# The modulation projections of a two-network kernel: all inputs summed in each column quarter, and the block turned on VectorE

## The chip, the cores and the metric

One Trainium2 chip, and one of its NeuronCores. The metric is the device time of one launch in microseconds, of the core that runs it. The kernel before took 2778.16 us (median of 3 runs, 2774.78 to 2778.19).

## The reference

Two small transformer-like networks run one after the other on the same 256 tokens of width 1024, all in fp32. The first has two layers (a gated feed-forward block, a mixer with three branches, a second gated feed-forward block). The second has two layers whose norms are shifted, scaled and gated by vectors made from a condition. The change touches only these vectors:

```python
def adaln(cond, w, b):
    return jnp.split(jax.nn.silu(cond) @ w + b, 6, axis=-1)
...
sh1, sc1, gt1, sh2, sc2, gt2 = [m[:, None, :] for m in adaln(c, w_ada, b_ada)]
csh1, csc1, cgt1, csh2, csc2, cgt2 = adaln(c_ctx, w_ada, b_ada)
```

`c` and `c_ctx` are two vectors of 1024, `w_ada` is 1024 x 6144 for each of two layers. So two rows are multiplied by 12,288 columns; the result is needed with the feature on the partition, since everything else in the kernel is kept that way.

## The kernel before, in words

Each engine has its own instruction list, written out by hand in the order in which it runs; semaphores tie them together. The sections are `load`, `one` (the first network, a loop over 2 layers), `cload`, `ctx`, `kv` and `two`.

The feed-forward blocks of section `one` are done by `multiply(c, which)`, twice per layer (`which` 0 and 1). Each walks through 17 groups of weights (k = 0 to 16; 11 for the way up, 6 for the way down) with a scheme that makes a 2 x 2 block product from 7 products instead of 8. A group's seven products ("quarters", all on L739) are on TensorE in this order: `middle(k)` has three, `raw(k+1)` two, `end(k)` two. Each quarter is 8 matmuls of 128 columns (6 on most of the way down), and each fp32 matmul shows as two passes in the profile, so a row of x16 is a whole quarter. VectorE makes the sums and differences of the weights that the products take (L1771, L1772, L1785, L1791), combines products (L1830 `c11_made`, L1845 `c22_made`, L1852 `c21_made`) and gates or adds the results. ScalarE copies products out of PSUM (L1337 is the line of its helper).

The modulation projections are strewn into these blocks: six in each `multiply`, at k = 1, 4, 7, 10, 13 and 16, so 12 per layer and 24 in all. One of them takes 512 of the 12,288 columns: its weights (2 MB, tile `fox_values_mla_qk_mla_values`, `vqv`) are 8 tiles of 128 inputs x 512 outputs, the condition (`cond_s`) is stationary as 8 tiles of 128 inputs x 32 columns of which two are real. Its steps are:

- TensorE, `ada_sums` (L710), between `middle(k)` and `raw(k+1)`: 8 matmuls of 512 columns. Input tile kt goes to column quarter kt mod 4 of the array, so each quarter of the PSUM partitions holds the sum over 2 of the 8 input tiles, for all 512 outputs.
- ScalarE, `ada_copy`: the 128 x 512 block is copied to SBUF (`ada_s`, in tile `delta_qkv`).
- TensorE, `ada_turn` (L719), after `end(k)`: 4 matmuls with a 128 x 128 piece of the block as the stationary operand and two columns of constants as the moving one; they add up the four quarters and turn the result at once.
- VectorE, `ada_bias` (L1756), last in iteration k: adds the bias into `modulation`.

SyncE's queue holds all the weight loads in one row. The load of a projection (`load_ada`, L565) stands just before the load of the group that shares its k (L595); the first of a layer stands between the loads of groups 0 and 1. It waits for a semaphore `ada_summed` that counts the finished sums; `load_ada` number 6 waits for another signal that the mixer sets. A signal's `at(c, k)` gives the semaphore and the count that k events of this layer stand for, on top of all earlier ones.

Of the kernel before, what the change touches and what calls it, by code (L numbers as in the profile page):

```python
# [21 lines left out]
ALU = mybir.AluOpType  # L22
# [4 lines left out]
P = 128  # L27
# [3 lines left out]
KD = D // P  # L31
# [232 lines left out]
def build(nc, stream, x_in, ctx_in, cond, positions, vec1, vec2, bada, consts, tables, out):  # L264
    with ExitStack() as ctx:
# [116 lines left out]
        ada_loaded = signal("ada_weights_loaded", one=16 * ADA_TURN)  # L382
        ada_summed = signal("ada_summed", 1, one=ADA_TURN)
        ada_copied = signal("ada_copied", one=ADA_TURN)

# [144 lines left out]
        def _(sp):  # L530
# [3 lines left out]
            sp.sem_inc(x_taken.handle, 2)  # L534
            for signal_ in (*lin_taken, *spot_taken, spot_ready, ada_summed, c11_made, c21_made):
                sp.sem_inc(signal_.handle, 1)
# [5 lines left out]
            for sec, (turns, groups) in SECTIONS.items():  # L542
# [19 lines left out]
                def load_ada(c, i, start):  # L562

                    sp.wait_ge(*(merged_made.at(c, 4) if i == ADAS else ada_summed.at(c, i)))
                    sp.dma_start(vqv[:, :], stream[bass.ds(start + places_["ada", i], P * FULL)].rearrange(  # L565
                        "(p w) -> p w", p=P)).then_inc(ada_loaded.handle, 16)
# [89 lines left out]
        def _(pe):  # L656
# [47 lines left out]
            def ada_sums(c, i):  # L704

                banks = free_spot(c, ("ada", i))
                pe.wait_ge(*ada_loaded.at(c, 16 * (i + 1)))
                for kt in range(KD):
                    q = kt % 4
                    mm = pe.matmul(banks[32 * q:32 * q + 32, 1, :], cond_s[:, kt, :], vqv[:, kt * 512:kt * 512 + 512],  # L710
                                   start=(kt < 4), stop=(kt >= 4))
                mm.then_inc(ada_summed.handle, 1)

            def ada_turn(c, i):

                pe.wait_ge(*ada_copied.at(c, i + 1))
                _, banks, _ = spot_of(c, ("ada", i))
                for m in range(4):
                    mm = pe.matmul(banks[:, 0, 2 * m:2 * m + 2], ada_s[:, i % 2, m * P:m * P + P],  # L719
                                   cst[:, C_TWO:C_TWO + 2], start=True, stop=True)  # L720
                mm.then_inc(spot_ready.handle, 1)

            def multiply(c, which):
# [70 lines left out]
                for k in range(count):  # L794
# [5 lines left out]
                    end(k)  # L800
                    if c.sec == "one" and k in ADA_AT:
                        ada_turn(c, ADAS * which + ADA_AT.index(k))
                if c.sec != "one" or which:
# [529 lines left out]
        def _(act_e):  # L1333
# [36 lines left out]

            def ada_copy(c, i):
                e_.wait_ge(*ada_summed.at(c, i + 1))
                if i >= 2:
                    e_.wait_ge(*spot_ready.at(c, SPOT[c.sec]["ada", i - 2][0][0] + 1))
                _, banks, _ = spot_of(c, ("ada", i))
                activate(ada_s[:, i % 2, :], banks[:, 1, :], ACT.Copy).then_inc(ada_copied.handle, 1)

            def two_halves(tile):
                return tile.rearrange("p (m t) -> p m t", m=2)

            def multiply(c, which):
# [12 lines left out]
                for k in range(count):  # L1394
# [6 lines left out]
                    activate(u4s[k % 2], mu_bank(c, which, k), ACT.Copy).then_inc(u4_kept.handle, 1)  # L1401
                    if c.sec == "one" and k in ADA_AT:
                        ada_copy(c, ADAS * which + ADA_AT.index(k))
                    if k + 1 < count:
# [299 lines left out]
        def _(ve):  # L1704
# [48 lines left out]
            def ada_bias(c, i):  # L1753
                banks, free = wait_spot(c, ("ada", i))
                m = bass.ds(c.turn * (4 * ADA_TURN) + 4 * i, 4)
                ve.tensor_tensor(mod[:, m, :], banks[:, 0, 0:8].rearrange("p (m j) -> p m j", m=4),  # L1756
                                 bias_a[:, m].unsqueeze(2).to_broadcast([P, 4, 2]), ALU.add).then_inc(free, 1)

# [740 lines left out]
```

## Time and profile before

| | |
|---|---|
| median of 3 runs | 2778.16 us (2774.78 to 2778.19) |
| the profiled execution | 2778.05 us, of which its span is 2776.3 us |
| granted TensorE clock, mean | 0.985 |
| TensorE matmul busy | 2684.1 us (97%) |
| VectorE, ScalarE busy | 1446.1 us (52%), 565.5 us (20%) |

"PE" is TensorE's matmul side, "PEld" its weight loads, which overlap the matmuls; DVE is VectorE, ACT ScalarE, SPq the queue of SyncE. A matmul's duration is from its start to its modelled end, and the next one starts well before that: steps between starts say what a matmul costs in a stream. In the names of tiles `spots` and `units` are PSUM.

### The profile page before, as it was taken

The page shows a single profiled execution, that of the slowest core. Times are in us where ns is not written, and L with a number is a line of the kernel's source. Part 1 is how long each engine was busy: PE and PEld are TensorE (multiplying, and loading weights), DVE is VectorE, ACT ScalarE, POOL GpSimd, SP SyncE. Part 2 cuts the span into 40 slices and gives each one's busy share as a digit, 9 for nine tenths or more (in the row PEclk, how much of TensorE's full clock was granted, in tenths as well). Part 3 has the DMA queues.
Part 4 walks back from the last instruction along what each step waited for, and adds up shares of the span by engine and source line. Part 5 has one row for each costly group of instructions (what it writes and reads, how often), then busy time and mean ns, then how long its engine had stood idle before and what let it go on. Part 6 is the DMA issues. An engine that isn't in the chain of part 4 may idle for free.

```text
span 2776.3 us, 49115 instructions
## 1 busy us (share of the span) xinstructions
PE 2684.1 (97%) x19874; PEld 2416.0 (87%) x19874; DVE 1446.1 (52%) x2397; ACT 565.5 (20%) x1165; POOL 8.5 (0%) x19
## 2 busy tenths in 40 slices
PE   7999999999999999999999999899997999988999
PEld 6999778988998999877988999769996689966999
DVE  6664254324765676225521666337662566625665
ACT  2111132111111111123211111232113321123111
POOL 0000000000000000000000000000000000000000
PEclk9999999999999999999999999999999999999999
DMA  6554321135556555431125556324443134432342
GB/s 252 217 201 172 114 107 47 48 135 211 188 208 229 188 199 208 152 114 61 47 77 191 209 213 223 133 91 148 157 152 151 68 125 180 159 120 87 125 180 107
DMA packets 50167, 415.98 MB, mean 150 GB/s; under 512 B 4016, under 2 KB 4272, under 8 KB 29584
## 3 DMA queue, kind: packets, MB, share of 16 engines
q1 hardware_dynamic: 49344, 409.34, 40.0%
q8 instruction: 163, 2.67, 0.4%
q0 software_dynamic: 592, 3.41, 0.3%
q14 instruction: 68, 0.56, 0.1%
HBM read 411.69 MB, written 1.05 MB: 149 GB/s over the span
## 4 chain that ended last, share of the span: by engine, by line
PE 94%; DVE 3%; issue 1%; ACT 1%; DVEq 1%; ACTq 0%
PE units L739 30%; PE spots L739 22%; PE units L680 20%; PE spots L1022 4%; PE units L1133 2%; PE spots L710 2%; PE units L1176 1%; PE units L1269 1%; PE units L827 1%; PE units L820 1%; PE spots L719 1%; PE spots L1210 1%; PE spots L1191 1%; PE spots L1200 1%; PE units L1172 1%
## 5 line engine op out<-in xcount | busy, mean ns | idle before, releaser
L680 PE MATMUL units<-normed,weights 128*128 128x256 f32 x1888 | 427.3, 385 | 18.6 <-ACT normed L1337 15.9
L680 PEld LDWEIGHTS units<-normed,weights 128*128 128x128 f32 x1888 | 359.9, 193 | 77.8 <-issue 13.6
L739 PE MATMUL units<-normed,weights 128*128 128x128 f32 x2176 | 273.3, 280 | 15.5 <-DVE normed L1720 9.3
L739 PEld LDWEIGHTS units<-normed,weights 128*128 128x128 f32 x2176 | 259.6, 195 | 29.1 <-issue 12.9
L739 PE MATMUL spots<-normed,weights 128*128 128x128 f32 x2176 | 267.5, 276 | 0.0
L739 PEld LDWEIGHTS spots<-normed,weights 128*128 128x128 f32 x2176 | 256.5, 194 | 0.0
L1337 ACT ACTIVATE mla_q_rope<-units 128x256 f32<-128x256 f32 (+1 forms) x248 | 95.5, 388 | 519.7 <-PE units L739 480.5
L1852 DVE TENSOR_TENSOR delta_new_values<-spots,mla_q_rope 128x256 f32<-128x256 f32 x116 | 49.2, 425 | 278.2 <-PE spots L739 278.2
L739 PE MATMUL units<-hidden,weights 128*128 128x128 f32 x1472 | 180.9, 276 | 0.0
L739 PE MATMUL spots<-hidden,weights 128*128 128x128 f32 x1472 | 180.1, 275 | 0.0
L739 PEld LDWEIGHTS units<-hidden,weights 128*128 128x128 f32 x1472 | 172.0, 192 | 6.7 <-issue 6.7
L739 PEld LDWEIGHTS spots<-hidden,weights 128*128 128x128 f32 x1472 | 172.1, 192 | 0.0
L1791 DVE TENSOR_TENSOR weights<-weights 128x1024 f32<-128x1024 f32 (+1 forms) x116 | 140.0, 1207 | 10.7
L739 PE MATMUL units<-squares,weights 128*128 128x128 f32 x1088 | 134.1, 276 | 6.5 <-DVE normed L1820 3.4
L1772 DVE TENSOR_TENSOR weights<-weights 128x1024 f32<-128x1024 f32 (+1 forms) x116 | 139.1, 1199 | 0.0
L739 PEld LDWEIGHTS units<-squares,weights 128*128 128x128 f32 x1088 | 126.9, 192 | 7.7 <-DVE weights L1785 7.7
L739 PE MATMUL spots<-squares,weights 128*128 128x128 f32 x1088 | 132.6, 275 | 0.0
L739 PEld LDWEIGHTS spots<-squares,weights 128*128 128x128 f32 x1088 | 127.0, 192 | 0.0
L680 PE MATMUL units<-hidden,weights 128*128 128x256 f32 x528 | 118.0, 381 | 0.4 <-DVE conv_in L2272 0.2
L680 PEld LDWEIGHTS units<-hidden,weights 128*128 128x128 f32 x528 | 99.1, 190 | 15.9 <-issue 1.5
L1337 ACT ACTIVATE silu_gate<-silu_gate 128x256 f32<-128x256 f32 (+1 forms) x90 | 38.0, 423 | 350.9 <-DVEq L1880 272.8
L1337 ACT ACTIVATE delta_state<-units 128x256 f32<-128x256 f32 x116 | 44.6, 384 | 261.3 <-PE units L739 261.3
(334 smaller groups left out, 3661.6 us busy)
## 6 DMA issues: line engine op xcount, KB each, us to landing
weights<-stream SPq DMA_DIRECT2D x140, 2048.0 KB, 7.7
values_mla_qk_mla_values<-stream SPq DMA_DIRECT2D x24, 2048.0 KB, 8.3
weights<-stream SPq DMA_DIRECT2D x46, 1024.0 KB, 5.1
weights<-stream SPq DMA_DIRECT2D x16, 768.0 KB, 5.4
constants<-consts SPq DMA_DIRECT2D x1, 1094.5 KB, 8.2
residual<-x_in SPq DMA_DIRECT2D x1, 1024.0 KB, 4.9
weights<-stream SPq DMA_DIRECT2D x4, 256.0 KB, 5.0
conv_in<-ctx_in POOLq DMA_DIRECT2D x1, 1024.0 KB, 9.1
```

What stands on the lines that cost most here:

```text
L680: mm = pe.matmul(dst, w[:, kt * width + col:kt * width + col + P], rhs[:, kt, :], start=(kt == 0), stop=(kt == k - 1))
L710: mm = pe.matmul(banks[32 * q:32 * q + 32, 1, :], cond_s[:, kt, :], vqv[:, kt * 512:kt * 512 + 512], start=(kt < 4), stop=(kt >= 4))
L719: mm = pe.matmul(banks[:, 0, 2 * m:2 * m + 2], ada_s[:, i % 2, m * P:m * P + P], cst[:, C_TWO:C_TWO + 2], start=True, stop=True)
L739: mm = pe.matmul(dst[:, m * P:m * P + P], weights[:, m, kt, :], moving(kt), start=(first and m == 0 and kt == 0), stop=(kt == n - 1), skip ...
L820: mm = pe.matmul(dst[:, m * T:m * T + T], w[:, col:col + P], mix_in[:, kt, :], start=(n == 0), stop=(n == KD - 1))
L827: mm = pe.matmul(dst, act[:, kt, part * P:part * P + P], w[:, kt * 512:kt * 512 + 512], start=(kt == 0), stop=(kt == KD - 1))
L1022: mm = pe.matmul(banks[:, e, p * P:p * P + P], lhs[:, t, e, p, :], rhs if turned else rhs[:, t, e, p, :], start=True, stop=True, is_transp ...
L1133: mm = pe.matmul(dst[:, m * T:m * T + T], w[:, col:col + P], merged[:, kt, :], start=(kt == 0), stop=(kt == KD - 1))
L1337: return nc.scalar.activation(dst, src, func, **kw)
L1772: ve.tensor_tensor(a21, a11, a21, ALU.subtract).then_inc(sums_made.handle, 1)
L1791: ve.tensor_tensor(a12, a12, a11, ALU.subtract).then_inc(sums_made.handle, 1)
L1852: ve.tensor_tensor(c2[:, :, tok0], halves_of(v_bank), halves_of(u2s[k % 2]), ALU.add).then_inc(c21_made.handle, 1)
```

## The change

Within a projection the work is dealt out differently. Each column quarter q of the array now gets all 8 input tiles, but only a quarter of the outputs: of each 128 outputs the 32 that begin at 32q, in four runs of 32. So there are 32 matmuls of 128 columns where there were 8 of 512; the sums over the inputs are complete in PSUM, as a 128 x 128 block. VectorE transposes that block in 32 x 32 pieces and adds the bias. The copy on ScalarE and the four turning matmuls are gone, and so are their two semaphores. The load of the next projection's weights now waits for the counter of all finished PSUM uses (`spot_ready`) at the value that the last projection's sums give it; for the first projection of a layer that is the value that all earlier sections and layers leave.

```diff
             def load_ada(c, i, start):

-                sp.wait_ge(*(merged_made.at(c, 4) if i == ADAS else ada_summed.at(c, i)))
+                before_ = SPOT["one"]["ada", i - 1][0][0] + 1 if i else 0
+                sp.wait_ge(*(merged_made.at(c, 4) if i == ADAS else spot_ready.at(c, before_)))
...
                 for kt in range(KD):
-                    q = kt % 4
-                    mm = pe.matmul(banks[32 * q:32 * q + 32, 1, :], cond_s[:, kt, :], vqv[:, kt * 512:kt * 512 + 512],
-                                   start=(kt < 4), stop=(kt >= 4))
-                mm.then_inc(ada_summed.handle, 1)
-
-            def ada_turn(c, i):
-
-                pe.wait_ge(*ada_copied.at(c, i + 1))
-                _, banks, _ = spot_of(c, ("ada", i))
-                for m in range(4):
-                    mm = pe.matmul(banks[:, 0, 2 * m:2 * m + 2], ada_s[:, i % 2, m * P:m * P + P],
-                                   cst[:, C_TWO:C_TWO + 2], start=True, stop=True)
+                    for q in range(4):
+                        w = vqv[:, kt * 512:kt * 512 + 512].rearrange("p (m c) -> p m c", m=4)[:, :, 32 * q:32 * q + 32]
+                        mm = pe.matmul(banks[32 * q:32 * q + 32, 0, 0:P], cond_s[:, kt, :], w, start=(kt == 0),
+                                       stop=(kt == KD - 1))
                 mm.then_inc(spot_ready.handle, 1)
...
-            def ada_copy(c, i):
-                e_.wait_ge(*ada_summed.at(c, i + 1))
...
-                activate(ada_s[:, i % 2, :], banks[:, 1, :], ACT.Copy).then_inc(ada_copied.handle, 1)
...
             def ada_bias(c, i):
                 banks, free = wait_spot(c, ("ada", i))
                 m = bass.ds(c.turn * (4 * ADA_TURN) + 4 * i, 4)
-                ve.tensor_tensor(mod[:, m, :], banks[:, 0, 0:8].rearrange("p (m j) -> p m j", m=4),
-                                 bias_a[:, m].unsqueeze(2).to_broadcast([P, 4, 2]), ALU.add).then_inc(free, 1)
+                ve.transpose(ada_s[:, i % 2, 0:P], banks[:, 0, 0:P]).then_inc(free, 1)
+                ve.drain()
+                turned = ada_s[:, i % 2, 0:P].rearrange("p (m j) -> p m j", m=4)[:, :, 0:2]
+                ve.tensor_tensor(mod[:, m, :], turned, bias_a[:, m].unsqueeze(2).to_broadcast([P, 4, 2]), ALU.add)
```

TensorE's list before, at k = 1 of a feed-forward block: the last quarter of `middle(1)`, the sums, `raw(2)`, `end(1)`, the turning products, and the first quarter of `middle(2)`.

```order
L739 MATMUL units<-squares,latents 128x128 x8
L671 ISA
L707 ISA
L710 MATMUL spots<-fox_values_mla_qk_mla_values,context_keys 32x512 x8
L757 REGISTER_ALU
L739 MATMUL units<-normed,weights 128x128 x8
L739 MATMUL spots<-normed,weights 128x128 x8
L739 MATMUL spots<-squares,weights 128x128 x8
L790 REGISTER_ALU
L739 MATMUL units<-normed,weights 128x128 x8
L716 ISA
L719 MATMUL spots<-constants,delta_qkv 128x2 x4
```

The same place now.

```order
L730 MATMUL units<-squares,latents 128x128 x8
L670 ISA
L706 ISA
L710 MATMUL spots<-fox_values_mla_qk_mla_values,context_keys 32x128 x32
L748 REGISTER_ALU
L730 MATMUL units<-normed,weights 128x128 x8
L730 MATMUL spots<-normed,weights 128x128 x8
L730 MATMUL spots<-squares,weights 128x128 x8
L781 REGISTER_ALU
L730 MATMUL units<-normed,weights 128x128 x8
L765 REGISTER_ALU
L730 MATMUL units<-squares,weights 128x128 x8
```

The sums stay where they were with four times the matmuls, and the four turning matmuls are gone from between `end(k)` and `middle(k+1)`.

VectorE's list before, at the end of the same iteration: the last two differences of the gated tile, the bias, and the first two instructions of the next iteration.

```order
L1890 TENSOR_TENSOR probabilities<-hidden,fox_qk 128x128
L1892 TENSOR_TENSOR probabilities<-hidden,probabilities 128x128
L1707 ISA
L1756 ISA [waits spot_summed]
L1756 REGISTER_ALU
L1756 TENSOR_TENSOR modulation<-spots,context_keys 128x8
L1830 TENSOR_TENSOR mla_k_rope<-spots,mla_q_rope 128x256 [waits c1_kept,product2_done]
L1835 TENSOR_TENSOR silu_gate<-mla_k_rope,rstd 128x256
```

The same place now.

```order
L1872 TENSOR_TENSOR probabilities<-hidden,fox_qk 128x128
L1874 TENSOR_TENSOR probabilities<-hidden,probabilities 128x128
L1687 ISA
L1736 STREAM_TRANSPOSE delta_qkv<-spots 128x128 [waits spot_summed]
L1739 ISA
L1739 REGISTER_ALU
L1739 TENSOR_TENSOR modulation<-delta_qkv,context_keys 128x8
L1812 TENSOR_TENSOR mla_k_rope<-spots,mla_q_rope 128x256 [waits c1_kept,product2_done]
L1817 TENSOR_TENSOR silu_gate<-mla_k_rope,rstd 128x256
```

One VectorE instruction and a drain are added ahead of the bias; what they wait for now comes from the sums instead of the turning products.

SyncE's list before, at the start of a layer: the loads of group 0, of the first projection, and of groups 1 and 2.

```order
L595 ISA [waits product3_done]
L595 DMA weights<-stream 128x4096
L564 ISA
L565 ISA [waits ada_summed]
L565 DMA fox_values_mla_qk_mla_values<-stream 128x4096
L571 REGISTER_ALU
L595 ISA [waits product3_done]
L595 DMA weights<-stream 128x4096
```

The same place now.

```order
L594 ISA [waits product3_done]
L594 DMA weights<-stream 128x4096
L563 ISA
L564 ISA [waits spot_summed]
L564 DMA fox_values_mla_qk_mla_values<-stream 128x4096
L570 REGISTER_ALU
L594 ISA [waits product3_done]
L594 DMA weights<-stream 128x4096
```

The order is the same and the semaphore another; the loads of groups 1 and 2 stand behind this wait.

## Rows read from the trace of the kernel before

**Rows 1.** Page: busy time by engine, and the chain that ended last by engine.
```profile
PE 2684.1 (97%) x19874; PEld 2416.0 (87%) x19874; DVE 1446.1 (52%) x2397; ACT 565.5 (20%) x1165; POOL 8.5 (0%) x19
PE 94%; DVE 3%; issue 1%; ACT 1%; DVEq 1%; ACTq 0%
```
**Rows 2.** Stretches, first feed-forward block: length; busy PE, PEld, DVE, ACT, POOL; clock; DMA.
```profile
27.00:250.00 223.00, 223.00 (x1972) 213.37 (x1973) 143.80 (x251) 36.76 (x83) 0.00 (x0) 1.00 0.55 202
```
**Rows 3.** Timeline around a projection: start, length, engine, line, operation, tiles, count.
```profile
43.09 1.95 PE L739 MATMUL units<-squares,latents 128*128 128x128 f32 x16
...
44.97 1.92 PE L710 MATMUL spots<-values_mla_qk_mla_values,context_keys 128*32 128x512 f32 x16
...
45.43 0.13 PEld L710 LDWEIGHTS spots<-values_mla_qk_mla_values,context_keys 128*32 128x32 f32 x4 [0.30 <-issue]
45.86 0.13 PEld L710 LDWEIGHTS spots<-values_mla_qk_mla_values,context_keys 128*32 128x32 f32 x4 [0.30 <-issue]
...
46.83 2.05 PE L739 MATMUL units<-normed,weights 128*128 128x128 f32 x16
...
52.18 1.87 PEld L739 LDWEIGHTS units<-normed,weights 128*128 128x128 f32 x16
...
53.97 0.97 PEld L719 LDWEIGHTS spots<-constants,delta_qkv 128*128 128x128 f32 x8
...
54.86 1.87 PEld L739 LDWEIGHTS units<-squares,weights 128*128 128x128 f32 x16
```
**Rows 4.** Timeline, TensorE: short matmuls on parts of the array, from narrow windows.
```profile
330.49 0.88 PE L936 MATMUL spots<-probabilities,values_mla_qk_mla_values 128*64 128x128 f32 x12
...
330.65 0.50 PE L936 MATMUL spots<-probabilities,values_mla_qk_mla_values 128*64 128x128 f32 x6
...
330.76 0.50 PE L936 MATMUL spots<-probabilities,values_mla_qk_mla_values 128*64 128x128 f32 x6
...
427.71 1.98 PE L998 MATMUL spots<-constants,rows 16*128 16x512 f32 x4
...
543.08 0.69 PE L1095 MATMUL spots<-probabilities,delta_new_values 128*64 128x64 f32 x16
```
**Rows 5.** Timeline: VectorE's own work, and the iteration behind the projection.
```profile
41.91 0.29 DVE L1887 TENSOR_TENSOR fox_qk<-hidden 128x128 f32<-128x128 f32 x1
...
57.76 0.17 DVE L1756 TENSOR_TENSOR modulation<-spots,context_keys 128x8 f32 x1
...
60.53 0.38 ACT L1337 ACTIVATE delta_state<-units 128x256 f32<-128x256 f32 x1 [1.28 <-PE units L739]
60.99 0.41 DVE L1845 TENSOR_TENSOR delta_new_values<-spots,delta_state 128x256 f32<-128x256 f32 x1
...
63.90 1.95 PE L739 MATMUL spots<-squares,weights 128*128 128x128 f32 x16
```
**Rows 6.** The first loads: timeline, a stretch of 13 us, DMA issues, the second layer's timeline.
```profile
16.14 0.38 ACT L1337 ACTIVATE rstd<-spots 128x256 f32<-128x256 f32 x1 [5.91 <-PE spots L695]
...
16.00:29.00 13.00, 7.47 (x51) 7.18 (x51) 11.84 (x24) 5.61 (x9) 0.00 (x0) 1.00 1.00 427
...
values_mla_qk_mla_values<-stream SPq DMA_DIRECT2D x24, 2048.0 KB, 8.3
...
30.23 1.22 DVE L1771 TENSOR_TENSOR latents<-weights 128x1024 f32<-128x1024 f32 x1
...
904.98 1.22 DVE L1771 TENSOR_TENSOR latents<-weights 128x1024 f32<-128x1024 f32 x1
```
**Rows 7.** Timeline between the two layers of the first network.
```profile
887.49 1.15 ACT L1337 ACTIVATE squares<-residual 128x512 f32<-128x512 f32 x2 [2.14 <-DVE residual L1795]
...
888.13 0.68 PE L695 MATMUL spots<-square_sums,ones 128*128 128x256 f32 x2
...
888.65 1.89 PE L701 MATMUL spots<-squares,ones 128*128 128x256 f32 x8
...
896.09 0.58 PE L739 MATMUL units<-normed,weights 128*128 128x128 f32 x1 [5.55 <-DVE normed L1720]
```

More of the change, by code:

```diff
@@ L382, in build @@
         ada_loaded = signal("ada_weights_loaded", one=16 * ADA_TURN)
-        ada_summed = signal("ada_summed", 1, one=ADA_TURN)
-        ada_copied = signal("ada_copied", one=ADA_TURN)
         p1_done, p2_done, p4_done, p5_done, p6_done, p7_done = (signal(f"product{i}_done", **MUS) for i in (1, 2, 4, 5, 6, 7))
@@ L534, in _ @@
             sp.sem_inc(x_taken.handle, 2)
-            for signal_ in (*lin_taken, *spot_taken, spot_ready, ada_summed, c11_made, c21_made):
+            for signal_ in (*lin_taken, *spot_taken, spot_ready, c11_made, c21_made):
                 sp.sem_inc(signal_.handle, 1)
@@ L800, in multiply @@
                     end(k)
-                    if c.sec == "one" and k in ADA_AT:
-                        ada_turn(c, ADAS * which + ADA_AT.index(k))
                 if c.sec != "one" or which:
@@ L1369, in res_root @@
                 root(summed(c)[1][:, :], banks[:, 0, 0:T], 1.0 / D, free).then_inc(res_rstd.handle, 1)
-            def ada_copy(c, i):
-                e_.wait_ge(*ada_summed.at(c, i + 1))
-                if i >= 2:
-                    e_.wait_ge(*spot_ready.at(c, SPOT[c.sec]["ada", i - 2][0][0] + 1))
-                _, banks, _ = spot_of(c, ("ada", i))
-                activate(ada_s[:, i % 2, :], banks[:, 1, :], ACT.Copy).then_inc(ada_copied.handle, 1)
             def two_halves(tile):
@@ L1401, in multiply @@
                     activate(u4s[k % 2], mu_bank(c, which, k), ACT.Copy).then_inc(u4_kept.handle, 1)
-                    if c.sec == "one" and k in ADA_AT:
-                        ada_copy(c, ADAS * which + ADA_AT.index(k))
                     if k + 1 < count:
```

## The prediction

> **What bounds the kernel now.** I read the page first. TensorE is busy 97% of the span and holds 94% of the chain that ended last [rows 1]; the reader is to see that whatever leaves TensorE's list shortens the run, unless another engine is then late. A busy PE is not proof, since matmul durations overlap, so I took the stretch of the first feed-forward block: 223.00 us long, PE busy 223.00, PEld 213.37, clock 1.00, while VectorE has 143.80 and ScalarE 36.76 [rows 2]. No gap is left there. Then the timeline of one projection [rows 3]: a whole quarter of 16 passes starts at 52.18 and the next thing at 53.97, so a full-array pass of 128 columns costs 1.79 / 16 = 0.112 us in the stream. All 24 projections stand in such stretches. So each edit on TensorE counts one for one, and those on VectorE, ScalarE and SyncE count only where they make TensorE late.
>
> **The turning products.** Their weight loads start at 53.97 and the next quarter's at 54.86 [rows 3]: 0.89 us for 8 passes of 0.11 us. They move only 2 columns each, but each needs 128 x 128 weights, and the loads set the pace. 24 x 0.89 = 21.4 us leave the list. Which of the 24 are on the path? 22 are followed by matmuls that wait for nothing (another quarter, or at the end of a first block the mixer's first projection): 22 x 0.89 = 19.6 us. The last of each layer is followed by the sums of squares (L695, L701). There L701 starts at 888.65; it takes ScalarE's squares, two instructions over 887.49 to 888.64, of which the first is done at about 888.1 [rows 7]. With the turn gone L695 starts 0.89 earlier (887.24) but L701 only at about 888.2: 0.45 us gained. In the second layer I take all of that 0.45. Between the layers the next matmul comes only at 896.09 [rows 7], 5.5 us after the last L701 ends, while the engines go back to the top of their loop; what sets that end may be VectorE, whose last instruction hardly moves, so 0 to 0.45, and I take 0.2. Sum: -20.25 us.
>
> **The sums.** Before: the preceding quarter's 16 passes start at 43.09 and would be through at 44.88; the first of L710 is at 44.97, the next quarter at 46.83 [rows 3]. Inside, the loads come in fours at 45.43 and 45.86: four quarters of the array run at once, and a round of four 512-column passes costs 0.43. So the block is four rounds, 1.86 us from its first start to the next quarter's, of which 0.1 is the switch back. After: 64 passes of 128 columns. If four run at once again these are 16 rounds. The trace has no such case; the nearest is L936, on halves of the array with the same 128 columns: rounds of two start at 330.49, 330.65, 330.76, so 0.16 for the first and 0.11 for each further one [rows 4]. 0.16 + 14 x 0.11 + (0.11 + 0.11 for the last with the switch) = 1.92 us, +0.06 each, 24 x 0.06 = +1.4 us. Both ends: the columns streamed are the same 4096 in four lanes, so below 1.86 there is nothing to gain but rounding (say -0.05). Above, the issue of instructions may bind, since a round of four now has 27 ns per pass: L1095 shows 16 passes of 64 columns within 0.69 us, of which the last one's own length is about 0.22, so 0.47 / 15 = 31 ns per pass [rows 4]; by that 64 passes take 1.98, with the switch 2.1 us, +0.24 each. With nothing overlapping the block takes 64 x 0.11 = 7.0 us. I take 1.92, as L936 is nearest in shape. The moving operand now has four runs of 32 values: L998, whose operand has four pieces (not one run), takes 1.98 us for 4 passes of 512, which is 4 x 0.43 plus a switch and the last one's tail [rows 4], so I cost pieces at nothing.
>
> The Trainium skill ("TensorEngine Tiling (Array Packing)", Instruction Overhead) puts about 60 cycles of overhead on each matmul, and "TensorE: Matmul & The Clock Gate" (Wait — 56ns, not 53.3ns?) a floor of about 25 ns from start to start, or about 62 ns where the sequencer's microcode handles each matmul. The floor agrees with the 31 ns of L1095 [rows 4] and leaves the sum as it is. Its 62 ns would be the case of slow issue under rival C; L1095's 31 ns speaks against it.
>
> **VectorE.** Before, 0.17 us for the bias (57.76). Now a transpose of 128 x 128 from PSUM, a drain and the same bias. The trace has no transpose. Nearest is a 128 x 128 fp32 instruction, 0.29 us [rows 5]; below nothing is excluded except that it can't beat the 0.17 of 128 x 8; above, if it ran at a quarter of that pace, 1.2 us. I take 0.3 plus 0.1 for the drain: +0.4 us, 24 times, 10 us of busy time. What hides it: the next iteration's c22 (L1845) is at 60.99, right after ScalarE's copy (60.53 + 0.38), and TensorE needs it for the quarter at 63.90 [rows 5]. Afterwards TensorE is 0.89 earlier (63.0) and VectorE 0.4 later (c22 done at 61.8): 1.2 us are left. So it costs nothing up to a transpose of about 1.5 us; beyond that each 0.1 us costs about 2 us in all. Queued behind it are c11 and the weight sums, which have more room. The Trainium skill ("VectorE: DVE Perf Modes", The three transpose paths) gives 311 ns for a bf16 block of this size, in 32 x 32 pieces; an estimate with it leaves the sum as it is.
>
> **ScalarE** loses 24 copies; it has only 36.76 us of work in 223.00 [rows 2], nothing waits for it there: 0.
>
> **SyncE.** The first projection's load of layer one had a wait that was met at once; now it waits for the first sum of squares, whose reader starts at 16.14 [rows 6]. The loads of groups 1 and 2 are queued behind it. A load of 2048 KB at 427 GB/s takes 4.9 us, and 8.3 from issue to landing, so 3.4 lie ahead of the data. Issued at 16.2, the projection's weights land at 24.5 and group 1 at 29.4; it is wanted at 30.23 by L1771 [rows 6]. 0.8 us to spare, and 2 more before TensorE would feel it. In the second layer the load waits for the end of L701 (888.65 + 1.89 = 890.5, [rows 7]) and group 1 is wanted at 904.98 [rows 6]: 14.4 us, against 14.0 at the start. I cost both at 0; if my landing times are 3 us short, each costs about 1 us.
>
> **Sum.** -20.25 + 1.4 = -18.85. The profiled execution took 2778.05 us (span 2776.3), 0.1 below the median of the runs: 2759.2 us.
>
> **The rivals.**
> - A, the forecast: 2759.2, own range 2755 to 2763.
> - B, issue binds: at 31 ns per pass the sums grow by 0.24 us: 24 x 0.24 = 5.8, so -14.5 and 2763.6. For it: 27 ns per pass is less than any stretch of the trace shows. Against it: L1095 has a 64-column round of 53 ns at least, so its 31 is mostly streaming, not issue.
> - C, slower than before: short passes on four quarters do not overlap four deep. The trace shows four at once only for long passes and two at once for short ones. Two at once: 32 rounds x 0.11 + 0.2 = 3.7 us, +1.87 x 24 = +45, net +25 and 2803. One by one: 7.2 us, +5.3 x 24 = +128, net +108 and 2886. It decides from 20.25 / 24 = 0.84 us more per projection, so from 2.7 us for L710, or 42 ns per pass. Issue at twice the 31 ns of L1095, so 62 ns, would be a case of it: 4.0 us, +2.1 x 24 = +51, net +31 and 2809; I give that 0.01 of C's chance. For C: the four streams now read interleaved pieces of the same tile at once. Against it: each old round also had four streams on that tile, and nothing in L936 suffers from two.
> - D, the gain turns into a wait: VectorE is late for c22, or the late loads of group 1 stop the start. For it: slack of only 1.2 us behind a transpose that no row prices. Against it: iterations without a projection have no turn either and the stretch has no gap [rows 2]. With a transpose of 2.3 us, 0.8 x 24 = 19 us are given back: 2778, no change.
>
> **Chances.** A 0.80, B 0.09, C 0.06, D 0.05 (spread from 2763 to 2779). A difference below 0.2% (5.6 us) can't be told from none here. Faster: A, B and over a third of D, 0.91; same 0.03; slower 0.06 (C). The range 2754 to 2766 takes A with the spread of the runs (one of three was 3.4 us under the median), and B; it leaves out C and most of D.
>
> **What would show it.** L719 and the ScalarE copy gone; L710 with 64 passes whose block, from its first start to the next quarter's, is 1.9 us (2.1: B; 2.7 or more: C). The quarter after `end(k)` follows within 0.11 us. The transpose 0.3 us, and no new wait of TensorE for c22. The first loads at 16.2 us, and no wait at 30.2. Busy time of TensorE down by about 19 us, of VectorE up by up to 10. It is wrong if L710 exceeds 2.1 us, or if TensorE shows gaps in the feed-forward blocks.

## The result: 2753.5 us, and what the profile after shows

The changed kernel took 2753.51 us (median of 4 runs, 2750.6 to 2757.75), the kernel before 2777.47 (4 runs): a ratio of 0.9915, interval 0.9903 to 0.9927. In two later comparisons it took 2753.12 and 2752.84. So it is 24 to 25 us faster. The forecast was 2759.2 with a range from 2754 to 2766: the time lies 5.7 us under the forecast and 0.5 us under the range.

The page of the kernel after, with the rows that answer to [rows 1] and the stretch that answers to [rows 2] (it ends 5 us earlier, as the mixer starts earlier):

```profile
span 2748.8 us, 50990 instructions
...
PE 2659.9 (97%) x20834; PEld 2422.0 (88%) x20834; DVE 1452.3 (53%) x2421; ACT 549.4 (20%) x1141; POOL 8.5 (0%) x19
...
PE 94%; DVE 3%; ACT 1%; issue 1%; DVEq 1%; DMA 0%; ACTq 0%; SPq 0%
```
```profile
27.00:245.00 218.00, 218.00 (x2213) 215.78 (x2214) 145.36 (x257) 32.46 (x77) 0.00 (x0) 1.00 0.58 211
```

TensorE is still without a gap in the feed-forward block and still has 94% of the chain. It has 960 instructions more (24 projections: 48 more passes, 8 turning passes fewer) and 24.2 us less busy time. ScalarE has 24 instructions fewer, VectorE 24 more. The timeline around the first projection, beside [rows 3] and [rows 5]; columns are start, length, engine, line, operation, tiles, count, and in brackets the idle time ahead and what ended it:

```profile
43.06 1.95 PE L730 MATMUL units<-squares,latents 128*128 128x128 f32 x16
...
44.94 1.96 PE L710 MATMUL spots<-values_mla_qk_mla_values,context_keys 128*32 128x128 f32 x64
...
46.82 2.05 PE L730 MATMUL units<-normed,weights 128*128 128x128 f32 x16
...
52.28 1.95 PE L730 MATMUL units<-normed,weights 128*128 128x128 f32 x16
...
54.07 1.95 PE L730 MATMUL units<-squares,weights 128*128 128x128 f32 x16
...
57.60 0.31 DVE L1736 STREAM_TRANSPOSE delta_qkv<-spots 128x128 f32<-128x128 f32 x1
...
58.23 0.17 DVE L1739 TENSOR_TENSOR modulation<-delta_qkv,context_keys 128x8 f32 x1 [0.32 <-issue]
...
61.47 0.41 DVE L1827 TENSOR_TENSOR delta_new_values<-spots,delta_state 128x256 f32<-128x256 f32 x1
...
63.00 1.17 PE L730 MATMUL spots<-squares,weights 128*128 128x128 f32 x9
```

Three things are to be seen. The block of 64 passes takes 46.82 - 44.94 = 1.88 us from its first start to the next quarter's, where 16 long passes took 1.86. The quarter at 52.28 is followed 1.79 us later by the next, with no turn between them. And the quarter that needs VectorE's sum c22 (L1827 now) starts at 63.00, where it was 63.90: TensorE is 0.90 us ahead and waits for nothing.

What the forecast did not have stands between the two layers, beside [rows 7]. In both sections a layer ends with the sums of squares; then the engines branch back to the top of their loop. First the chain of waits, of the kernel before and of the kernel after (start, length, what held it):

```profile
888.69 5.25 issue
```
```profile
878.83 2.73 issue
```

"issue" is time in which VectorE waits for nothing that the profile shows: it is on its way back to the loop's first instruction. 5.25 us became 2.73. TensorE has a branch of its own, whose duration the trace gives; before, then after (shortest, median and longest of two in ns, and the starts of the first and the last):

```profile
L1319 PEldq COMPARE_BRANCH  x2: 83/3364/6645, 888.8 to 1765.0; - x2
```
```profile
L1308 PEldq COMPARE_BRANCH  x2: 82/1822/3562, 879.0 to 1741.9; - x2
```

It took 6.65 us and takes 3.56. In both kernels it is what ends last: TensorE is through its branch at 895.4 before and 882.6 after, and its first matmul follows at 896.09 and 883.21, 0.6 us behind; VectorE's first product was there at 894.5 and 882.2. The bracket [5.55 <-DVE normed L1720] names the last semaphore, not the branch.

The next rows are from the queue statistics (packets, MB, share of the 16 engines): of the kernel before over 888.6 to 892.2, then of the kernel after over 878.7 to 879.8, both from VectorE's branch to the start of the first packet of instructions. Queues q8 and q14 carry instructions. By their volume q8 is TensorE's (the change adds 1,920 instructions to TensorE and 8 packets of 16 KB to q8) and q14 that of the other engines.

```profile
q1 hardware_dynamic: 105, 1.52, 98.9%
q14 instruction: 1, 0.01, 0.5%
```
```profile
q14 instruction: 1, 0.01, 2.7%
```

Then the timeline of the kernel after, and the last row from r9_after2, a second trace of the same kernel:

```profile
880.54 0.35 SPq L564 DMA_DIRECT2D values_mla_qk_mla_values<-stream  x1
...
881.14 1.00 SPq L594 DMA_DIRECT2D weights<-stream  x2
881.81 2.19 DVE L1700 TENSOR_SCALAR normed<-residual,vectors 128x256 f32<-128x256 f32 x8 [2.98 <-issue]
...
883.21 2.76 PE L730 MATMUL units<-normed,weights 128*128 128x128 f32 x16 [2.84 <-DVE normed L1700]
...
887.95 1.28 ACT L1326 ACT_TABLE_LOAD   x1 [6.66 <-issue]
...
889.24 0.38 ACT L1326 ACTIVATE mla_q_rope<-units 128x256 f32<-128x256 f32 x1
...
889.86 0.37 PE L730 MATMUL units<-squares,weights 128*128 128x128 f32 x1 [1.19 <-DVE normed L1802]
```
```profile
889.96 0.37 PE L730 MATMUL units<-squares,weights 128*128 128x128 f32 x1 [3.14 <-ACT mla_q_rope L1326]
```

Before, SyncE issued the three loads of the next layer from 884.8 on, ahead of the loop-back. VectorE branched at 888.63, and the first packet on q14 started at 892.12, 3.5 us later; until then the weights had 98.9% of the DMA engines' time. TensorE's packet on q8 started at 892.96. After, the first load waits for the sums of squares that end the layer and is issued at 880.54. VectorE branches at 878.76, the first packet on q14 starts at 879.79, only 1.0 us later, and that on q8 at 880.05. The packets themselves take 0.3 to 1.2 us in the two kernels, and VectorE and TensorE go on 1.3 to 1.5 us after the end of theirs. So what the loads cost is the wait of a packet for its start. TensorE's idle time went from 5.55 [rows 7] to 2.84 us.

ScalarE branches last (880.95) and now meets the loads: the next packets on q14 start only at 885.33 and 886.04, and it has 6.66 us of "issue". Its copy at 889.24 is late for TensorE's third quarter. The bracket there names VectorE's L1802, but in r8 below the same quarter starts before L1802 is done; the quarter starts 0.24 us after the end of the copy here as in the row of r9_after2, which names ScalarE. The weight sum that the quarter needs besides was done at 889.23, so about 0.6 of the 1.19 us are ScalarE's. From the end of the sums of squares to the third quarter of the new layer it is 890.54 to 901.67 = 11.1 us before and 880.38 to 889.86 = 9.5 after: 1.6 us are won there.

In the second network too the gap shrank, by 2.9 us, without a load being moved. Before, then after, the first matmul of its second layer with the idle time ahead of it:

```profile
2447.13 1.22 PE L680 MATMUL units<-normed,weights 128*128 128x256 f32 x2 [8.27 <-ACT normed L1337]
```
```profile
2421.68 1.64 PE L679 MATMUL units<-normed,weights 128*128 128x256 f32 x3 [5.40 <-ACT normed L1326]
```

### The profile page after: what moved, and what is told of

It reads as the page before. It is cut to its first block, busy times and chain, and to the rows that moved or that the text cites. A ratio compares the mean times of both kernels' runs of the same rounds, so it can differ in the third digit from the quotient of the medians.

```text
span 2748.8 us, 50990 instructions
## 1 busy us (share of the span) xinstructions
PE 2659.9 (97%) x20834; PEld 2422.0 (88%) x20834; DVE 1452.3 (53%) x2421; ACT 549.4 (20%) x1141; POOL 8.5 (0%) x19
## 3 DMA queue, kind: packets, MB, share of 16 engines
HBM read 411.69 MB, written 1.05 MB: 150 GB/s over the span
## 4 chain that ended last, share of the span: by engine, by line
PE 94%; DVE 3%; ACT 1%; issue 1%; DVEq 1%; DMA 0%; ACTq 0%; SPq 0%
PE units L730 30%; PE spots L730 22%; PE units L679 20%; PE spots L1011 4%; PE units L1122 2%; PE spots L710 2%; PE units L1165 1%; PE units L1258 1%; PE units L816 1%; PE units L809 1%; PE spots L1199 1%; PE spots L1180 1%; PE spots L1189 1%; PE units L1161 1%; PE spots L885 0%
## 5 line engine op out<-in xcount | busy, mean ns | idle before, releaser
L1767 DVE TENSOR_TENSOR weights<-latents,weights 128x1024 f32<-128x1024 f32 (+1 forms) x56 | 67.5, 1206 | 49.9 <-PE units L730 49.1
```

Source lines behind the costliest of these rows:

```text
L1767: ve.tensor_tensor(a11, mu_sum(c, k), a11, ALU.subtract).then_inc(sums_made.handle, 1)
```

## The experiments

Two theories for the 5.7 us below the forecast were set against each other and against chance (C, that only the stretches at half clock fell otherwise). L (late loads): the engines fetch their instructions through the same DMA engines as the weights, so a load issued at a loop-back slows the return, and loads that are later free it. V (code layout of VectorE): VectorE's list has other instructions in it, so its pieces fall elsewhere in the blocks that are fetched, and VectorE no longer stands waiting for one of them in the second network. Ratios are to the kernel before, in runs of the same chip.

| run | us (runs) | ratio, interval | TensorE idle between layers, net 1 / net 2 |
|---|---|---|---|
| before (profiled) | 2778.05 | 1 | 5.55 / 8.27 |
| r1_after | 2753.12 (5) | 0.9911, 0.9897 to 0.9925 | 2.87 / 5.34 |
| r2_early_load | 2754.42 (5) | 0.9919, 0.9906 to 0.9933 | 5.65 / 5.24 |
| r3_before_late_load | 2778.11 (11) | 0.9999, 0.999 to 1.0008 | 2.72 / 9.35 |
| r4_before_pad | 2773.23 (11) | 0.9982, 0.9973 to 0.9991 | 5.05 / 5.31 |
| r5_keep_turn | 2773.74 (10) | 0.9982, 0.9973 to 0.9992 | 2.81 / 5.89 |
| r6_quarter_by_quarter | 2852.59 (1) | 1.027, no interval | 2.69 / 5.35 |
| r7_six_transposes | 2772.23 (10) | 0.9978, 0.9968 to 0.9987 | 6.36 / 5.32 |
| r8_rstd_load | 2752.81 (5) | 0.9914, 0.99 to 0.9928 | 2.85 / 5.37 |
| r9_after2 | 2752.84 (4) | 0.9907, 0.9892 to 0.9922 | 2.96 / 5.43 |
| r10_after_pad | 2755.26 (5) | 0.9918, 0.9904 to 0.9932 | 3.22 / 5.66 |
| r11_two_late_loads | 2750.78 (4) | 0.9901, 0.9886 to 0.9916 | 2.84 / 3.13 |
| r12_rstd_both | 2748.07 (4) | 0.9893, 0.9878 to 0.9908 | 3.23 / 2.69 |

**r1_after and r9_after2**: the changed kernel again, no edit.

> The changed kernel itself, as the base of this group. All theories: about 24 us under the kernel before (2753.5 measured, 2759.2 forecast). The turning products and the sums account for -20.3 + 24 x 0.03 = -19.6 us. Theory L (late loads): of the rest, about 2.6 us come from the end of the first network's first layer, where the loop-back of TensorE takes 3.6 us in place of 6.6. Theory V (code layout of VectorE): about 2.8 us come from the end of the second network's first layer, where VectorE no longer stops for 5.1 us after its loop-back. Theory C (clock): the rest is chance, from where the stretches at half clock fall; then this profile should show other low-clock stretches than the first one and a time anywhere in 2750 to 2758.

> The changed kernel again, as the base of this group: 2753 us. If the half-clock stretches are chance, their sum in this profile lies between the 65 us and the 82 us of the two earlier ones, and the time follows it by about a quarter of the difference.

Both gaps came back (2.87 and 5.34, 2.96 and 5.43), so they belong to the kernel. What does not is the time at half clock: by the granted clock (twice what it lacks to 1, times the span) the stretches at 1.2 GHz add up to 82 us before, 65 after, 82 in r1_after and 65 in r9_after2, with profiled spans of 2748.8, 2753.4 and 2750.9 for the last three. Traces of one kernel differ by as much as the two first traces do, so that part of their difference can't be put down to the change. What a stretch costs depends on where it falls: lined up matmul by matmul, r1_after loses 3.3 us to r9_after2 around 400 to 443, where it has 6.9 us more at half clock, so about half; 10.2 us more at 1858 cost 1.8.

**r2_early_load**: the changed kernel with the old moment for a layer's first load.

```diff
-                    before_ = SPOT["one"]["ada", i - 1][0][0] + 1 if i else 0
+                    before_ = SPOT["one"]["ada", i - 1][0][0] + 1 if i else -1
```

> The changed kernel, but the first projection load of a layer waits only until the last projection of the layer before is summed, as the kernel before does; so this load and those of groups 1 and 2 are issued before the end of a layer again. Theory L: the weight transfers are under way when the engines go back to the top of their loop; TensorE's loop-back takes 6 to 7 us again and VectorE's 5 us in place of 2.8, and the kernel is 1.5 to 3 us slower than the changed one. Rival (V or C): the loop-back time does not depend on the loads; no difference over 0.5 us.

Its timeline between the layers of the first network:

```profile
877.60 0.33 SPq L594 DMA_DIRECT2D weights<-stream  x1
...
884.04 2.19 DVE L1700 TENSOR_SCALAR normed<-residual,vectors 128x256 f32<-128x256 f32 x8 [5.46 <-issue]
885.77 2.42 PEld L730 LDWEIGHTS units<-normed,weights 128*128 128x128 f32 x11 [6.05 <-DVE normed L1700]
885.77 2.50 PE L730 MATMUL units<-normed,weights 128*128 128x128 f32 x10 [5.65 <-DVE normed L1700]
```

With the loads back ahead of the branch (the first is issued at 874.76), VectorE's return is 5.46 again (before 5.48), TensorE's own branch takes 6.38 and TensorE idles 5.65. From the last matmul of layer 1 to the second mixer it takes 227.7 us, in the three traces of the changed kernel 225.2 to 225.7: L is shown in the trace, 2.0 to 2.5 us. The medians differ by 1.3 us, below the 1.5 to 3 expected, and their intervals don't tell it from none.

**r3_before_late_load**: the kernel before with only that load moved.

```diff
-                    sp.wait_ge(*(merged_made.at(c, 4) if i == ADAS else ada_summed.at(c, i)))
+                    sp.wait_ge(*(merged_made.at(c, 4) if i == ADAS else ada_summed.at(c, i) if i else spot_ready.at(c, 0)))
```

> The kernel before, but the first projection load of a layer waits for all earlier PSUM sums, as the changed kernel does. Theory L: the loop-back of TensorE between the layers shrinks from 6.6 to about 3.6 us; 1.5 to 3 us faster than the kernel before, so 2774.5 to 2776. Rival (V or C): within 0.5 us of the kernel before.

```profile
892.27 0.35 SPq L565 DMA_DIRECT2D values_mla_qk_mla_values<-stream  x1
...
893.28 2.19 DVE L1720 TENSOR_SCALAR normed<-residual,vectors 128x256 f32<-128x256 f32 x8 [3.02 <-issue]
...
894.83 3.50 PE L739 MATMUL units<-normed,weights 128*128 128x128 f32 x16 [2.72 <-DVE normed L1720]
...
900.07 1.28 ACT L1337 ACT_TABLE_LOAD   x1 [7.04 <-issue]
...
901.98 2.05 PE L739 MATMUL units<-squares,weights 128*128 128x128 f32 x16 [1.69 <-DVE squares L1821]
```

The gap falls by itself from 5.55 to 2.72, again with VectorE's return at 3.02 and TensorE's own branch at 3.82, and again ScalarE pays (7.04). From the last matmul of layer 1 to the second mixer 1.2 us are left. The median shows none of the 1.5 to 3 us that were expected; in the trace the second network's gap was 9.35, 1.1 longer than before. So L holds for the gap, and its worth in the whole is one to two microseconds, less than these runs can tell. VectorE's code is that of the kernel before here, and the long gap of the second network is still there.

**r4_before_pad**: the kernel before with two more instructions on VectorE, 24 times, that do nothing.

```diff
             def ada_bias(c, i):
+                ve.drain()
+                ve.drain()
```

> The kernel before with two more drain instructions of VectorE ahead of each of the 24 bias additions: 24 instructions more in the loop's code, about as many as the changed kernel has, and at most 0.1 us of VectorE's time each. Theory V: the stop of 5.1 us of VectorE behind its loop-back in the second network goes (it depends on where the code falls in the fetched blocks), and the kernel is 2 to 3 us faster. Rival (L or C): the stop stays, no difference over 0.5 us.

The first matmul of the second network's second layer:

```profile
2442.52 27.27 PE L680 MATMUL units<-normed,weights 128*128 128x256 f32 x112 [5.31 <-ACT normed L1337]
```

Work was added and the kernel became 5 us faster (0.9982, interval below 1; 2 to 3 were expected): the gap is 5.31 in place of 8.27. V is shown. The change itself adds as many instructions to VectorE, 48 with the drains. In the trace of before, the chain of waits has the piece that went:

```profile
2439.98 0.04 DVEq L2332
...
2440.08 5.07 issue
2445.15 0.05 DVEq L2174
```

VectorE was back from its branch and stood 5.07 us with nothing to wait for; a packet came in on q14 at 2443.31, and VectorE went on 1.5 us after its end, as it does after a branch. The number of packets is not what changed: r4 and the kernel after have one on q14 at the same place (2442.07, 2420.82), but VectorE isn't waiting for it. In the kernel after, the chain goes from 2417.53 to the next instruction at 2417.66. TensorE was through its own branch at 2443.70 and could have started then, so of the 5.07 us 3 show as a longer gap. Lined up matmul by matmul, the profiled r4 is 5.1 us shorter than before: 3.1 at this gap, and 2.0 net elsewhere, most of it at places where one of the two is at half clock (72 us in all against 82).

**r10_after_pad**: the same two instructions in the changed kernel.

```diff
             def ada_bias(c, i):
+                ve.drain()
+                ve.drain()
```

> The changed kernel with two more drain instructions of VectorE per projection. Theory V says that only the place of VectorE's code in the fetched blocks matters: the gap of TensorE between the layers of the second network stays at 5.7 us unless the 24 instructions move a block's edge again; then it is 8 to 9 us and the kernel 3 us slower. Rival (the drains or the transposes themselves shift something in time): 0.1 us x 24 slower at most, and no new gap.

The second network's gap stays (5.66); the 2.4 us over r9_after2 are within what 78 us at half clock, against 65, and the intervals allow. So there is room for these 48 instructions before the costly place comes back.

**r5_keep_turn**: the changed kernel with a turn's worth of passes put back (their result goes nowhere).

```diff
+            def ada_turn(c, i):
+
+                _, banks, _ = spot_of(c, ("ada", i))
+                for m in range(4):
+                    mm = pe.matmul(banks[:, 1, 2 * m:2 * m + 2], ones[:, :],
+                                   cst[:, C_TWO:C_TWO + 2], start=True, stop=True)
                 mm.then_inc(spot_ready.handle, 1)
...
+                    if c.sec == "one" and k in ADA_AT:
+                        ada_turn(c, ADAS * which + ADA_AT.index(k))
```

> The changed kernel with the four turning products of each projection kept in their old place on TensorE, as work whose result is not used (a constant tile as the stationary operand, into the unused PSUM bank). VectorE waits for them again. The sum of the prediction: 0.89 us for each of 24, of which two are mostly hidden behind ScalarE's squares, so 20 us slower than the changed kernel (2773 if that is at 2753). Rival (the gain came from the loads and the code layout, and the turning products were hidden): under 5 us slower.

```profile
52.27 1.95 PE L737 MATMUL units<-normed,weights 128*128 128x128 f32 x16
54.05 0.95 PE L717 MATMUL spots<-constants,ones 128*128 128x2 f32 x8
54.86 2.03 PE L737 MATMUL units<-squares,weights 128*128 128x128 f32 x16
```

The 8 passes take 0.81 us, and the quarter behind them 0.08 more than one behind another quarter, so 0.89 as forecast. The run is 20.6 us longer than r1_after: the turn's price of 20.25 stands. VectorE waits for the turn here too, so the run keeps both of its effects. What is left of the gain (4.2 us) is what r2 and r4 explain (about 1.6 and 3), less the 0.7 of the sums.

**r6_quarter_by_quarter**: the loops of `ada_sums` exchanged, so that neighbours in the list are on the same quarter of the array.

```diff
-                for kt in range(KD):
-                    for q in range(4):
+                for q in range(4):
+                    for kt in range(KD):
```

> The changed kernel with the two loops of the sums exchanged: all 8 inputs for column quarter 0, then for quarter 1, and so on. The same 32 matmuls, but neighbours share a quarter. If the overlap comes from neighbours being in different quarters (rival C of the prediction as a mechanism), 64 passes run one after the other at 0.11 us: 7.0 us per projection in place of 1.9, and the kernel is 24 x 5.1 = 122 us slower, 2875. If TensorE reorders across quarters by itself, no change.

```profile
44.94 5.95 PE L710 MATMUL spots<-values_mla_qk_mla_values,context_keys 128*32 128x128 f32 x64
50.83 1.38 PE L730 MATMUL units<-normed,weights 128*128 128x128 f32 x10
```

The same 64 passes take 5.9 us in place of 1.88, so 92 ns a pass in place of 29, and the whole is 99 us longer in its one run (24 x 4.0 = 96; 122 were expected at 0.11 a pass). Rival C's mechanism is real; the order of the list keeps it away.

**r7_six_transposes**: VectorE turns each block six times, to find the slack.

```diff
+                for _ in range(5):
+                    ve.transpose(ada_s[:, i % 2, 0:P], banks[:, 0, 0:P])
+                    ve.drain()
```

> The changed kernel with the transpose done six times (each with its drain) in place of once: 5 x (0.31 + about 0.3) = 2 to 3 us more of VectorE's time per projection. The prediction's slack: c22 has 1.1 us to spare (c22 at 61.47 + 0.41, TensorE's quarter at 63.00), so TensorE waits 1 to 2 us per projection, 24 to 45 us in all. Rival (VectorE has the 2.3 us of waits of each iteration as slack, and nothing is given back): under 3 us slower.

```profile
57.44 1.88 DVE L1737 STREAM_TRANSPOSE delta_qkv<-spots 128x128 f32<-128x128 f32 x5
...
63.26 0.42 DVE L1830 TENSOR_TENSOR delta_new_values<-spots,delta_state 128x256 f32<-128x256 f32 x1
63.73 0.94 PE L730 MATMUL spots<-squares,weights 128*128 128x128 f32 x6 [0.73 <-DVE delta_new_values L1830]
```
```profile
PE spots L730 <- DVE delta_new_values L1830: 15.7, 19, 1.1
```

Five more transposes make VectorE 59.39 - 57.44 = 1.95 us later. The quarter starts at 63.73 in place of 63.00, in a trace that is 0.17 us ahead up to there, so 0.90 late. So about 1.05 us of slack was there. The table of waits has 19 such waits, 15.7 us (2.8 in the changed kernel): 12.9 us of the 19 by which the kernel is longer. Lined up with r1_after, 16 of the 24 places lose 17.3 us in all, 1.1 each, and the other 8 nothing; so the price stayed under the 24 to 45 us expected, which took every place as alike. Another 3.5 are the first network's gap, 6.36 again: VectorE now reaches its branch after the loads are issued, at 889.1, and its return takes 5.5 us. Here it is VectorE that ends last; TensorE's own branch, before the loads, took 3.5.

**r8_rstd_load**: the changed kernel, a layer's first load still later, so that ScalarE is back too.

```diff
-                    sp.wait_ge(*(merged_made.at(c, 4) if i == ADAS else spot_ready.at(c, before_)))
+                    sp.wait_ge(*(merged_made.at(c, 4) if i == ADAS else spot_ready.at(c, before_) if i else res_rstd.at(c, 0)))
```

> The changed kernel, but the first projection load of a layer waits for ScalarE's last instruction of the layer before (the reciprocal root), about 1 us later than now. Theory L in its second part: in the changed kernel ScalarE's loop-back (at 880.95) collides with the loads (issued at 880.54 to 881.8) and takes 6.8 us, and TensorE waits 1.5 us for its copy at 889.9. With the loads 1 us later ScalarE is back in about 3 us, that wait goes, and the kernel is 0.5 to 1.5 us faster than the changed one. Rival: the loads are still in its way, no difference in ScalarE's 6.8 us.

```profile
883.11 2.05 PE L730 MATMUL units<-normed,weights 128*128 128x128 f32 x16 [2.85 <-DVE normed L1700]
883.54 1.28 ACT L1326 ACT_TABLE_LOAD   x1 [2.37 <-issue]
...
889.18 1.05 PE L730 MATMUL units<-squares,weights 128*128 128x128 f32 x7 [2.24 <-DVE weights L1767]
```

ScalarE's return fell from 6.66 to 2.37 us, and the time is that of r1 and r9, not the 0.5 to 1.5 us less that were expected: VectorE's own list (norms, weight sums, squares) runs with hardly a hole from 881.71 to the weight sum L1767 that TensorE needs, done at 889.12, and is next in line. So 8.9 us pass from the sums of squares to that quarter, after 9.5 in the changed kernel: 0.6 us, less than the runs can tell.

**r11_two_late_loads and r12_rstd_both**: in the second network, loads 1 and 2 of a layer wait for the last PSUM sum of the layer before (r11); both networks wait for `res_rstd` (r12). The edit of r11 where `load` is called (`load` itself gets one more wait):

```diff
-                            load(n, l * size + base, before(Place(sec, l), n))
+                            load(n, l * size + base, before(Place(sec, l), n),
+                                 spot_ready.at(Place(sec, l), 0) if sec == "two" and n in (1, 2) else None)
```

> The changed kernel, and in the second network too the loads of groups 1 and 2 of a layer wait for the last sum of the layer before. Theory L: TensorE's gap between the layers there, 5.7 us, shrinks by 1 to 3 us, as between the layers of the first network (6.0 to 3.2). Rival: that gap is VectorE's and ScalarE's chain of norms and stays at 5.7; no change over 0.5 us.

> The changed kernel with both: in each network the loads that stand at a layer's start wait for ScalarE's last root of the layer before. Theory L: 1.5 to 4 us faster than the changed kernel, 2749 to 2751.5. Rival: the loads come too late for their first readers and the gain is given back; no change or slower.

TensorE in r12, across the same place:

```profile
2415.45 2.06 PE L703 MATMUL spots<-squares,ones 128*128 128x256 f32 x8
2420.20 1.12 PE L682 MATMUL units<-normed,weights 128*128 128x256 f32 x4 [2.69 <-ACT normed L1329]
```

The gap is 3.13 and 2.69, from 5.43. r11 is 2.1 us under r9_after2, r12 4.8, and all runs of r12 (2746.44 to 2749.45) lie under all of r9 (2750.33 to 2754.08), though the intervals of their ratios overlap. r12 is the fastest kernel of the study, 2748.07 us, 30 under the kernel before. Lined up matmul by matmul, its trace is 6.3 us shorter than that of r9, and 5.7 of it lie at this boundary: 2.7 are the gap, and the other 3 are 14 matmuls behind it that r9 has at half clock and r12 has not (mean granted clock over 2414 to 2440: 0.87 and 1.00). Whether the shorter gap keeps the clock up isn't shown: in the first network gaps of 2.9 us come with and without a stretch at half clock behind them (r1 and r9).

## Why the prediction was right in kind and short in size

**What bounds the kernel.** Right: each microsecond taken from TensorE's list shortened the run.

**The turning products, -20.25.** Right. The turn's 0.89 us are gone at 22 places. At the end of the first layer the last quarter and the second sum of squares start at 876.18 and 878.38, 2.20 apart, where they were 885.98 and 888.65, 2.67: 0.47 gained, 0.45 forecast. The sums of squares then take 2.00 in place of 1.89, so 0.36 are left at their end. r5 gives the price back as 20.6.

**The sums, +1.4.** Right, and half of it: the blocks take 1.88 us, +0.03 in place of +0.06, so +0.7. A quarter on its own needs what r6 shows; taking turns, four of them need 29 ns a pass. Rival B (31 ns, 2.1 us) and rival C are refuted, and so is the case of C at 62 ns. The Trainium skill's floor ("TensorE: Matmul & The Clock Gate", Wait — 56ns, not 53.3ns?), which the prediction gave as about 25 ns from start to start, agrees with the 29 ns.

**VectorE, 0.** Right. The transpose is 0.31 us, the bias follows 0.32 us after its end, and c22 starts at 61.47, 0.48 later than in [rows 5]; 0.4 was forecast. r7 put the slack at 1.05 us, where 1.2 was forecast, and showed that TensorE waits beyond it. Rival D did not come.

**ScalarE, 0.** Right within the blocks; between the layers its return, 6.66 us, costs TensorE about 0.6 us (r8), which the forecast didn't have.

**SyncE, 0, and the gaps taken as fixed: the step that failed.** The prediction asked only whether the loads would be too late. They were not (the load is issued at 16.24 and TensorE has no wait at 30). It did not ask what a load does to its neighbours: moved past the loop-back, it left the DMA engines free while two engines fetched their instructions. And it took the 5.5 us between the layers as fixed ("0 to 0.45"). It named the way back to the top of the loop, but priced nothing in it, though the chain of before has 5.25 us of "issue" there. r2 and r3 showed that half of the gap was the loads; the boundary as a whole gave 1.6 us.

**A term that was missing, and the larger one.** The forecast put nothing for the code of VectorE. The second network's gap of 8.27 us held 3 us that depend on where that code lies. The change moved it; r4 moved it alone.

**The sum of the profiled executions**, 2778.05 to 2750.6, -27.45. Lined up matmul by matmul, the work gives -19.6 (22 x 0.86, and 0.34 at each layer's end), the first network's boundary -1.6 and the second network's gap -3.1: together -24.3. The other -3.2 lie elsewhere, most of it where one of the two traces is at half clock, above all -1.8 at 1301 to 1334 and -1.75 at 2551 to 2576 of the kernel before; in all it has 82 us at half clock against 65. r1 and r9 show that this differs between traces of one kernel. The medians differ by 24 to 25 us, as the -24.3 without it.

**The range.** Its lower end took the forecast less the spread of three runs. The step of 0 for SyncE had been bounded on the side of a loss alone (1 us each), and nothing stood for the return of the engines or for the place of the code.

## What to carry to other kernels

Passes on different parts of the array overlap only if neighbours in the list are on different parts: put the loop over the parts innermost. Look at what the DMA queues carry where engines branch back, for a load that can wait some 6 us there may be worth more than an early one (one to three microseconds at each such place here). The bracket of a wait names a semaphore; look at the branch of the waiting engine itself too. And a gap of "issue" with nothing waited for is not a constant: 48 instructions more on one engine moved it by 3 us, so a change of a few microseconds should be tried beside the old kernel with only its code moved.

## What the runs showed of the hardware

A loop-back cost VectorE 3.0 us with idle DMA engines and 5.5 with weight loads in flight (r2, r3), TensorE's branch 3.6 and 6.4 to 6.6 (after, r2, before), ScalarE 2.4 and 6.7 to 7.1 (r8, after, r9). The first instruction packet behind VectorE's branch started 1.0 us after it with idle DMA engines and 3.5 us after it with loads in flight (r3, r2). Where its code lies cost VectorE 5 us more behind one branch, 3 of them on TensorE (before, r4). 64 passes of 128 columns on four 32-column quarters took 1.88 us in turns and 5.9 us one quarter after the other. VectorE turned 128 x 128 fp32 values out of PSUM in 0.31 us. What sets the time at half clock, 61 to 82 us in kernels with nearly the same work, stays open.
